# A two-layer hybrid decoder step on one core: the gate-vector product and the l2 norms moved behind one more block

## The reference: what is computed

```python
x += 0.5 * swiglu(rms(x))                       # FFN 1, width 2816
u  = rms(x) @ w_in                              # qkv of DeltaNet (1536), z, b, a, q, k, v, two gates
ya = gated_deltanet(conv4(u_qkv), z, b, a)      # 4 heads of 128, chunks of 64; samples: one recurrent step
yb = diff_attention(q, k, v)                    # 4 heads, two score maps each; samples: over the paged cache
x += (sigmoid(g_a) * (ya @ w_a) + sigmoid(g_b) * (yb @ w_b)) @ w_o
x += 0.5 * swiglu(rms(x))                       # FFN 2
x += sigmoid(rms(x) @ w_ple_gate) * (p @ w_ple)
```

## Time and profile before

| | us |
|---|---|
| median of 3 executions (lowest, highest) | 3003.37 (3002.32, 3007.3) |
| the profiled execution, its own time | 3012.68 |
| its span, first to last instruction | 3010.9 |
| PE busy in the span | 2836.5 (94%) |
| DVE, ACT, POOL busy | 1496.4, 1026.4, 1120.7 |
| mean granted clock of TensorE | 0.951 of full |

### The profile page before, as it was taken

How to read it: one execution, slowest core, us unless ns; L and a number is a source line. 1 busy time by engine, 2 the same in 40 slices (tenths; PEclk the granted TensorE clock), 3 DMA queues, 4 the chain that set the end, 5 groups by cost and what they waited for, 6 DMA issues and landing times.

```text
span 3010.9 us, 56500 instructions
## 1 busy us (share of the span) xinstructions
PE 2836.5 (94%) x23634; PEld 2665.3 (89%) x23634; DVE 1496.4 (50%) x1425; ACT 1026.4 (34%) x1153; POOL 1120.7 (37%) x352
## 2 busy tenths in 40 slices
PE   6999998979989899999989999989898998999996
PEld 6999998956579899999989999988564998999996
DVE  4444256734566554442554432666254765444335
ACT  4343233211255233332343332342123643433222
POOL 3545343220033345544435544432200333555432
PEclk9999999986889999999999999999878999999998
DMA  3222232165532222222322222322645222222221
GB/s 133 89 92 76 96 122 80 68 189 152 157 105 80 83 84 98 95 73 91 105 70 92 90 82 88 124 77 98 190 147 163 85 85 85 84 98 83 82 91 65
DMA packets 119360, 304.55 MB, mean 101 GB/s; under 512 B 14898, under 2 KB 24882, under 8 KB 118706
## 3 DMA queue, kind: packets, MB, share of 16 engines
q1 hardware_dynamic: 119218, 302.54, 30.7%
HBM read 291.05 MB, written 11.44 MB: 100 GB/s over the span
## 4 chain that ended last, share of the span: by engine, by line
PE 75%; issue 13%; DVE 4%; POOL 3%; SPq 3%; DMA 1%; ACT 1%; DVEq 1%; POOLq 0%; ACTq 0%
PE ps L570 51%; PE ps L613 11%; POOL wlo L1404 3%; SPq L396 1%; SPq L394 1%; PE ps L948 1%; PE ps L947 1%; PE ps L893 1%; PE ps L762 1%; DVE Hl L1900 1%; PE ps L648 1%; PE ps L864 1%; PE ps L938 1%; PE ps L924 1%; PE ps L911 1%
## 5 line engine op out<-in xcount | busy, mean ns | idle before, releaser
L1404 POOL TENSOR_TENSOR wlo<-raw,whi 128x2048 fp32r<-128x2048 f32 (+1 forms) x224 | 949.8, 4240 | 1521.2 <-ACT whi L1108 1521.0
L570 PE MATMUL ps<-Hh,whi 128*128 128x260 f32 x3456 | 695.1, 283 | 39.6 <-DVE Hl L1087 22.2
L570 PE MATMUL ps<-Hl,whi 128*128 128x260 f32 x3456 | 694.4, 282 | 0.0
L570 PE MATMUL ps<-Hh,wlo 128*128 128x260 f32 x3456 | 693.0, 282 | 0.0
L1108 ACT ACTIVATE whi<-raw 128x2048 fp32r<-128x2048 f32 (+1 forms) x224 | 395.7, 1766 | 695.3 <-PE ps L570 606.0
L570 PEld LDWEIGHTS ps<-Hh,whi 128*128 128x128 f32 x3456 | 531.0, 189 | 42.1 <-issue 40.8
L570 PEld LDWEIGHTS ps<-Hl,whi 128*128 128x128 f32 x3456 | 533.8, 189 | 0.0
L570 PEld LDWEIGHTS ps<-Hh,wlo 128*128 128x128 f32 x3456 | 532.8, 189 | 0.0
L1479 DVE TENSOR_TENSOR tb<-tb,ta 128x520 f32<-128x520 f32 x88 | 346.3, 3936 | 202.9 <-ACT ta L1108 202.5
L570 PE MATMUL ps<-Gh,whi 128*128 128x260 f32 x1408 | 284.3, 283 | 6.7 <-POOL Gl L1418 6.7
L570 PE MATMUL ps<-Gh,wlo 128*128 128x260 f32 x1408 | 283.2, 282 | 0.0
(11 more groups left out here) (265 smaller groups left out, 3670.5 us busy)
## 6 DMA issues: line engine op xcount, KB each, us to landing
raw<-in_ffn_up SPq DMA_DIRECT2D x176, 512.0 KB, 4.3
raw<-in_ffn_down SPq DMA_DIRECT2D x128, 352.0 KB, 3.2
kb<-in_cache_k SPq DMA_DIRECT2D x128, 256.0 KB, 3.1
kb<-in_cache_v SPq DMA_DIRECT2D x128, 256.0 KB, 3.0
raw<-in_w_in SPq DMA_DIRECT2D x56, 512.0 KB, 4.4
raw<-in_w_gate SPq DMA_DIRECT2D x32, 512.0 KB, 4.5
raw<-in_w_ab SPq DMA_DIRECT2D x16, 512.0 KB, 4.2
raw<-in_w_o SPq DMA_DIRECT2D x16, 512.0 KB, 4.2
```

The lines of the kernel that those rows point to most:

```text
L570: last = nc.tensor.matmul(ps[:, bank + 2 * m + c, 0:HT], w, x[:, k0 + k, c * HT:(c + 1) * HT], start=starts and k == 0 and n == 0, stop=st ...
L1404: nc.gpsimd.tensor_tensor(wlo[:, p, 0:cols], raw[:, p, 0:cols], whi[:, p, 0:cols].bitcast(F32), ALU.subtract).then_inc(split_done, 1)
```

## The change

In words: PE runs block 45 right behind block 44 and only then the `w_ba` product; every sum of squares, the `BA` transposes, `gcum` and `sab` move behind one more block. DVE evicts block 44 ahead of the samples' convolution, and its norms and small steps stand one `low_u` later. ACT's `hi` calls move the same way. SP no longer waits for block 51 for all of the mixer's first loads: key tiles 0 and 1 go when block 50 is done, `st1` when in addition `lo` of block 50 is done, `st0` when block 51 is done, and then key tiles 2 and 3. The diff:

```diff
@@ -425,6 +425,10 @@
                 for n in range(n0, n1):
                     load(L, n, n % 2, A["w_in"][L, n - B_IN])
 
+            def state_load(L, b):
+                sp_.dma_start(st[b][:, :, :], A["state_delta"][L, 4 * b:4 * b + 4].rearrange("s h k v -> k s h v")
+                              ).then_inc(st_load[b], 16)
+
             def state_store(L, b):
 
                 sp_.wait_ge(s_dve.sem, s_dve.at(f"o{b}3", L))
@@ -460,12 +464,15 @@
                 sp_.wait_ge(evac, L * NE + 42 + FREE)
                 sp_.dma_start(O["kv"][L], U[:, U_K:U_K + 2 * H, :]).then_inc(kv_out, 16)
 
+                sp_.wait_ge(block_done, L * NB + (B_GATE - 1 + FREE))
+                for t in range(2):
+                    cache_pages(sp_, A["cache_k"], L, t)
+                sp_.wait_ge(split_done, L * NB + (B_GATE - 1 + FREE))
+                state_load(L, 1)
                 sp_.wait_ge(block_done, L * NB + (B_GATE + FREE))
-                for t in range(4):
+                state_load(L, 0)
+                for t in range(2, 4):
                     cache_pages(sp_, A["cache_k"], L, t)
-                for b in range(2):
-                    sp_.dma_start(st[b][:, :, :], A["state_delta"][L, 4 * b:4 * b + 4].rearrange("s h k v -> k s h v")
-                                  ).then_inc(st_load[b], 16)
                 for t in range(4, 16):
 
                     sp_.wait_ge(q_pe.sem, q_pe.at(f"k{t - 4}", L))
@@ -669,23 +676,24 @@
                     last.then_inc(l_pe.sem, 1)
 
                 block_low(L, 44, 36, 0)
+                block_low(L, 45, 37, 1)
 
                 pe.wait_ge(t_pool.sem, t_pool.at("w", L))
-                pe.wait_ge(evac, L * NE + (36 + FREE))
+                pe.wait_ge(evac, L * NE + (37 + FREE))
                 for k in range(KD):
                     for n, (w, x) in enumerate(((wbah, Hh), (wbah, Hl), (wbal, Hh))):
                         for c in range(2):
                             last = nc.tensor.matmul(ps[:, 4 + c, 0:HT], w[:, k, :], x[:, k, c * HT:(c + 1) * HT],
                                                     start=k == 0 and n == 0, stop=k == KD - 1 and n == 2)
                 last.then_inc(t_pe.on("ba", L), 1)
-                block_low(L, 45, 37, 1, mid=lambda: l2_sum(0, 0))
+                block_low(L, 46, 38, 2, mid=lambda: l2_sum(0, 0))
                 for t in range(4):
                     tr(ps[:, 6, t * 8:t * 8 + 8], BA[:, t * P:(t + 1) * P], 8)
                 tr(ps[0:NSEQ, 6, 32:40], BA[:, SEQ:T], 8).then_inc(t_pe.on("tok", L), 1)
                 l2_sum(0, 1)
-                block_low(L, 46, 38, 2, mid=lambda: l2_sum(1, 0))
+                block_low(L, 47, 39, 3, mid=lambda: l2_sum(1, 0))
                 l2_sum(1, 1)
-                block_low(L, 47, 39, 3, mid=lambda: l2_sum(2, 0))
+                block_low(L, 48, 40, 4, mid=lambda: l2_sum(2, 0))
                 l2_sum(2, 1)
                 pe.wait_ge(t_dve.sem, t_dve.at("g", L))
                 pe.wait_ge(cm_load, L * 16 + 16)
@@ -696,14 +704,13 @@
                     last = nc.tensor.matmul(ps[:, 7, 32 + 16 * b:48 + 16 * b], CM[:, M_HALF + P * b:M_HALF + P * (b + 1)], gv,
                                             start=True, stop=True)
                 last.then_inc(t_pe.on("gcum", L), 1)
-                block_low(L, 48, 40, 4, mid=lambda: l2_sum(3, 0))
+                block_low(L, 49, 41, 5, mid=lambda: l2_sum(3, 0))
                 l2_sum(3, 1)
                 pe.wait_ge(t_dve.sem, t_dve.at("sexp", L))
 
                 pe.wait_ge(t_dve.sem, t_dve.at("bt", L))
                 nc.tensor.matmul(ps[:, 6, 64:128], CC[0:NSEQ, C_ONE:C_ONE + P], sexp[:, :, :, :].rearrange("p a s h -> p (a s h)"),
                                  start=True, stop=True).then_inc(t_pe.on("sab", L), 1)
-                block_low(L, 49, 41, 5)
                 block_low(L, 50, 42, 6)
 
                 def decay(G):
@@ -1194,8 +1201,9 @@
                 act.drain()
                 l2_squares(0)
                 hi(L, 46, 0, 23)
+                hi(L, 47, 1, 23)
                 l2_root(0, 0)
-                hi(L, 47, 1, 23)
+                hi(L, 48, 0, 24)
                 l2_root(0, 1)
                 l2_squares(1)
                 act.wait_ge(t_dve.sem, t_dve.at("bt", L))
@@ -1207,11 +1215,11 @@
                 act.drain()
                 A_(sp[:, :, :], sp[:, :, :], ACT.Ln, bias=1.0).then_inc(t_act.on("softplus", L), 1)
                 l2_root(1, 0)
-                hi(L, 48, 0, 24)
+                hi(L, 49, 1, 24)
                 l2_root(1, 1)
                 l2_squares(2)
                 l2_root(2, 0)
-                hi(L, 49, 1, 24)
+                hi(L, 50, 0, 25)
                 l2_root(2, 1)
                 l2_squares(3)
                 act.wait_ge(t_dve.sem, t_dve.at("kdx", L))
@@ -1220,9 +1228,8 @@
                 A_(dl[:, :, :, :].rearrange("p b t h -> p (b t h)"), ps[:, 7, 32:64], ACT.Exp).then_inc(t_act.on("decays", L), 1)
                 A_(sp[0:NSEQ, 4, :], gg[0:NSEQ, 4, :], ACT.Exp).then_inc(t_act.on("asam", L), 1)
                 l2_root(3, 0)
-                hi(L, 50, 0, 25)
+                hi(L, 51, 1, 25)
                 l2_root(3, 1)
-                hi(L, 51, 1, 25)
 
                 def decay(G):
                     act.wait_ge(d_pe.sem, d_pe.at(f"e{G}", L))
@@ -1594,6 +1601,7 @@
                         V.scalar_tensor_tensor(out=U[:, i + 4 * p, :], in0=U[:, i + 4 * p, :], scalar=1.0 if p else P ** -0.5,
                                                in1=ta[:, p, :], op0=ALU.mult, op1=ALU.mult).then_inc(l_dve.sem, 1)
 
+                low_u(0)
                 dve.drain()
                 dve.wait_ge(sc_load, L * 16 + 16)
                 TT(csam[:, :, :], rawtail[:, :, 3:11], taps(3), ALU.mult)
@@ -1606,10 +1614,10 @@
                         dve.drain()
                 last.then_inc(t_dve.on("csam", L), 1)
                 V.memset(bt[:, :, :], 0.0)
-                low_u(0)
+                low_u(1)
                 dve.wait_ge(t_pe.sem, t_pe.at("ba", L))
                 TT(halves(BA[:, :]), ps[0:2 * H, 4:6, 0:HT], halves(R[0:2 * H, :]), ALU.mult).then_inc(t_dve.on("ba", L), 1)
-                low_u(1)
+                low_u(2)
                 dve.wait_ge(t_pe.sem, t_pe.at("tok", L))
                 V.tensor_copy(bt[:, 0:4, :], ps[:, 6, 0:32].rearrange("p (t c) -> p t c", c=8))
                 V.tensor_copy(bt[0:NSEQ, 4, :], ps[0:NSEQ, 6, 32:40]).then_inc(t_dve.on("bt", L), 1)
@@ -1618,7 +1626,7 @@
                 dve.drain()
                 V.tensor_scalar(gg[:, :, :], ax[:, :, :], 0.0, None, ALU.max)
                 l2_norms(0)
-                low_u(2)
+                low_u(3)
                 dve.wait_ge(t_act.sem, t_act.at("softplus", L))
                 TT(gg[:, :, :], gg[:, :, :], sp[:, :, :], ALU.add)
                 dve.drain()
@@ -1628,7 +1636,7 @@
                 V.tensor_scalar(nlam[:, :], bcast[:, L:L + 1], -1.0, None, ALU.mult)
                 V.tensor_scalar(negb[:, :, :], beta[:, 0:4, :], -1.0, None, ALU.mult)
                 l2_norms(1)
-                low_u(3)
+                low_u(4)
                 dve.wait_ge(t_pe.sem, t_pe.at("gcum", L))
                 V.tensor_copy(gcs[:, :, :], ps[:, 7, 0:16].rearrange("p (c h) -> p c h", h=H))
                 dve.drain()
@@ -1641,11 +1649,10 @@
                 for n, x in enumerate((sp, beta)):
                     last = TT(sexp[:, n, :, :], x[0:NSEQ, 4, :].unsqueeze(1).broadcast_to([NSEQ, NSEQ, H]), id8, ALU.mult)
                 last.then_inc(t_dve.on("sexp", L), 1)
-                low_u(4)
+                low_u(5)
                 l2_norms(3)
                 dve.wait_ge(t_pe.sem, t_pe.at("sab", L))
                 V.tensor_copy(sab[:, :, :, :].rearrange("p a s h -> p (a s h)"), ps[:, 6, 64:128]).then_inc(t_dve.on("sab", L), 1)
-                low_u(5)
 
                 def gates(G):
                     return grid(Zx[:, :]), gg[:, 2 * G:2 * G + 2, :]
```

## The result

| | before | changed |
|---|---|---|
| median, us (lowest to highest) | 3005.34 (3002.32 to 3012.16, 4 runs) | 2958.56 (2956.08 to 2962.09, 4 runs) |
| ratio to before, 95% interval | | 0.9842 [0.9821, 0.9863] |
| the profiled execution, its time and span | 3012.68, 3010.9 | 2960.26, 2958.5 |
| mean granted clock | 0.951 | 0.960 |

The change takes 46.8 us off the median. Both waits that it is about are gone from PE. The view of waits of PE in the changed kernel, window 480 to 800 (line, what it waited for: total, times, longest us), answers to the earlier trace rows.

What follows compares the result with a forecast made beforehand. PE, busy 94% of the span, bounds the kernel, so only its idle time and clock can be had. Gains 10.8 + 3.0 + 25.3 + 6.4 = 45.5 us from 3003.4 give 2958; range 2943 to 2974.

Steps and rivals of the forecast that it cites:

- Block 45 ahead of the product: At the `w_ba` product: a 2.4 us gap replaces waits of 7.7 and 7.9 us, gaining 10.8 us.
- The clock in the product: `w_ba` product at full clock, 5.72 us instead of 8.29; less 1.1 a layer at block 45, gain 3.0 us.
- The small work one block later: Norms and small steps up to `decay(0)` and block 51: just fits, `bk` 0.2 us; 0 taken, bounds 0 to 3.8 lost.
- SP's order: State loads around block 51: `st0` goes out at its end, lands with 5 us of cover; 25.3 us wait gone.
- The clock in the read: First state read to `key(0)`: 11.6 us instead of 14.8, gaining 3.2 a layer, 6.4 in all.
- Rival 2: Last key tile to first gate block: the clock gives or takes later; 2967 to 2986, or 2948; chance 0.12 either side.
- forecast case: Whole kernel: all terms hold, 45.5 us gained, 2958 us, own range 2950 to 2968; chance 0.74.
- the first: State loads: `st0` queues behind `st1`, so the stall only shrinks, PE standing 3 us a layer; 2970; chance 0.06.
- the fourth: From the read to the gates: clock could stay at 1.2 GHz, making it slower, 3078 with 60 us a layer; chance 0.03.
- the fifth: At the `w_ba` product: the wait reappears behind block 45, ACT or POOL being late; 2972; chance 0.03.
- The third: Low-clock windows around product and read: the clock gives more, 28.8 us where the sum has 9.4; 2938.5; chance 0.02.

Runs made afterwards that it cites:

- conv_first: Changed kernel with DVE doing the samples' convolution before evicting block 44 (`low_u(0)`), as before the change; 2964.71 us, 0.9877 of before.
- half_evict: Changed kernel with half 0 of block 44 evicted before the last tap of block 43; median 7.7 us from the changed kernel's on one chip, overlapping intervals.
- order_only: Changed kernel with the new PE, DVE and ACT orders but SP's old mixer loads; share of the gain 0.54%.
- states_first: Changed kernel with SP waiting for block 51 for everything, then issuing `st0` first, nothing early; 2962.94 us, 0.9854 of before.
- st0_late: Changed kernel with `st0` issued behind key tiles 2 and 3; 2969.01 us, 0.9880 of before.
- mixed_read: Changed kernel with the first state read's matmuls mixed into `invert_first(0)` and the second's into `key(8)`; 2958.95 us.
- half_evict_first_mixed: Changed kernel with half 0 of block 44 evicted before block 43's last tap and only the first state read mixed into `invert_first(0)`; median 2951.9 us.
- loads_only: Kernel before with only SP's new loads, and the old orders of PE, DVE and ACT; share of the gain 1.14%.

## Why the prediction was right

Forecast 2958, measured 2958.6. Point by point, by its own steps:

- **Block 45 ahead of the product**: a gap of 2.4 us was forecast in both layers, 2.4 and 2.6 came. `conv_first` (4.7 and 5.0) and `half_evict` (0.4 and 0.6) move it as DVE's work behind the taps says.
- **The clock in the product**: 5.7 us forecast, 5.76 measured. The loss at the start of block 45 was put at 1.1 us a layer. In the twelve layers with this gap (changed kernel twice, `order_only`, `states_first`, `st0_late`, `mixed_read`) the low time was 0 in four, 3.4 in six and 6.8 in two; the stretch took 101.4, 102.9 and 104.4 us on average, so the mean loss is 1.2 a layer; in the changed kernel's trace it was 0 and 1.5. Together with the gap 13.8 us were forecast, 13.6 came in the profile.
- **The small work one block later**: the cover of 0.8 us at `decay(0)` was there to 0.1 (574.39 against 575.16), `bk` took 0.19, and PE waited for neither `Zx` nor `U` around block 51.
- **SP's order**: the wait of 25.3 us went. The landing was taken as 8.24 us, it was 6.4 to 7.2, and the cover is 6 to 7 us instead of 5. The forecast gave no share to the early tiles and `st1`; `states_first` shows that they have none.
- **The clock in the read**: 3.2 us a layer were forecast. The second stretch shrank by 14.2 and 17.3, less the waits of 12.6 and 12.7 that is 1.6 and 4.6: 6.2 against 6.4. The mean was right and the picture only in part: in layer 0 the clock fell inside the read (4.83 us instead of 3.7), in layer 1 right behind it.
- **Slips that did not enter the sum.** The tile at 696.46 was called the last; it is `key(14)`, and the last one starts at 705.8. So "57" for `key(0)` to `key(15)` is the time to `key(14)`; the whole stretch took 67.3 and 62.9 us before and takes 64.5 and 63.9 now. Rival 2 took its 155.0 and 145.5 from the same tile: from `key(15)` on the layers differ by 5.2 us (145.8 and 140.7), not by 9.5. I also said that the SP chain bounds the stretch to `key(15)`. The changed kernel's layer 0 has no wait for a tile in it at all, so it hangs on PE's own steps as much. And the bounds of the single terms add up to 2952 to 2976, not to the forecast case's own range of 2950 to 2968.
- **The rivals**: the first, the fourth and the fifth did not come. Of the second, the clock in the later stretches, 7.7 us came in the profiled pair, 7.0 of them in layer 0. There the wait of 2.4 us for tile 14 has gone, behind which the clock was at 1.2 GHz for 51.2 us in the kernel before; in the changed kernel it falls behind `key(15)` instead, for 34.1 us. That the wait made the difference is likely from this, not shown. Between the medians 1.3 us more than the forecast remain. The third (2938) was not seen: of the 61 us of low time in the first two stretches of before 48 went, and the gain beyond the shorter waits is 9 us. PE was idle in 29 of these 48 us, which are counted in the waits already, and busy in 19; half of 19 is 9.6. The Trainium skill ("TensorE: Matmul & The Clock Gate", Terms) would price these 48 at 24, an estimate by its rule; the measurement decides for less.

Right for the reason given, then, though the agreement to 1 us is partly luck. The median of before came out at 3005.3 instead of 3003.4, and the last stretch, which the change leaves alone, takes 134 to 147 us in the traces of this study. The 9.3 us taken off to get from the profiled execution to the median were not shown either: the profiled one of the changed kernel stands only 1.7 above its median.

## What to carry to other kernels

When a queue issues many loads behind one release, look at which of them is wanted first and what its issue time plus landing leaves; here the place of one load ahead of 16 key DMAs was worth about 30 us in two layers, and sending the rest early nothing that could be measured. A wait of PE on a small product can often be filled with the next big block, but then the wait moves to the banks of that block: evict them ahead of whatever DVE does next, by halves if one half is done early. And count a stall at more than its length where PE restarts at the lower clock: 2.5 us of wait cost 5.5 in `st0_late`.

## What the runs showed of the hardware

- With one and the same gap of 2.4 to 2.6 us in dense matmuls, the granted clock stayed at 2.4 GHz in four layers of twelve, all of them in layer 0, and fell for 3.4 or 6.8 us in eight; each 3.4 us of it cost 1.3 to 1.6 us. Behind gaps of 0.4 to 0.6 us it never fell there (8 layers, four traces of three kernels).
- Behind PE's wait of 2.4 to 2.7 us for tile 14, among matmuls of 64 to 512 columns, the clock fell in four layers of four: for 51.2 us in three of them (kernel before, `order_only`, `half_evict_first_mixed`), with PE busy in over 50 of them, and for 10.2 us in `st0_late`.
- 32 matmuls of 2 columns as a block, 3.7 us without any idle time at full clock: wherever the clock was up at their start, it fell within them or up to 1.4 us behind them. With three quarters of the first read's spread in `invert_first(0)` it stayed up in five layers of six; with three quarters of the second's spread in `key(8)` it fell among them in three of four, for 6.8 to 20.5 us.
- DVE's product `bk` of 32 columns took 4.61 us beside POOL's conversion (kernel before and `loads_only`, both layers) and 0.19 us alone (changed kernel and `order_only`).
